# RWKV time mix: the low-rank inputs mixed by scaled factors, gates and decays between the wide projections

## The reference

```python
xx = _token_shift(h) - h
xr, xw, xk, xv, xa, xg = [h + xx * mu[i] for i in range(6)]
r, k, v = xr @ w_r, xk @ w_k, xv @ w_v                      # 1024 x 1024 each
w = -softplus(-(w0 + tanh(xw @ w1) @ w2)) - 0.5             # w1: 1024 x 64
a = sigmoid(a0 + (xa @ a1) @ a2)                            # a1: 1024 x 64
g = sigmoid(xg @ g1) @ g2                                   # g1: 1024 x 160
kk = heads(k * k_k); kk = kk / max(norm(kk), 1e-12)
k = k * (1 + (a - 1) * k_a)
decay = exp(-exp(w))
# scan over time with r, decay, k, v, -kk, kk * a; group norm over heads;
# plus sum(r * k * r_k) * v; times g; times w_o
```

## Time and profile before

| | |
|---|---|
| median of 3 runs | 1948.68 us (1945.17 to 1950.43) |
| the profiled execution's own time | 1943.3 us |
| its span in the trace | 1941.5 us |
| mean granted TensorE clock | 0.957 |
| RWKV part up to the head work | about 1462 to 1608 us of the span |

### The profile page before, as it was taken

How to read it: one execution, slowest core, us unless ns; L and a number is a source line. 1 busy time by engine, 2 the same in 40 slices (tenths; PEclk the granted TensorE clock), 3 DMA queues, 4 the chain that set the end, 5 groups by cost and what they waited for, 6 DMA issues and landing times.

```text
span 1941.5 us, 29831 instructions
## 1 busy us (share of the span) xinstructions
PE 1770.4 (91%) x12438; PEld 1271.5 (65%) x12438; DVE 917.8 (47%) x1344; ACT 672.9 (35%) x950; POOL 499.5 (26%) x362
## 2 busy tenths in 40 slices
PE   5989999999769999999999589889997979969998
PEld 2889997795534444444444366668885749958887
DVE  4286623677712112121222665464456775765553
ACT  3454347442301112111111344444334443334342
POOL 1268887100133445454453100000000001400000
PEclk9999999999879999999999788889998989999999
DMA  8545551166599998979888532155444500023442
GB/s 357 183 151 181 195 178 63 66 239 255 237 426 423 419 381 326 393 297 421 354 333 350 205 110 107 55 200 189 180 181 144 194 22 25 4 87 147 180 178 102
DMA packets 64970, 414.41 MB, mean 213 GB/s; under 512 B 20612, under 2 KB 20628, under 8 KB 24528
## 3 DMA queue, kind: packets, MB, share of 16 engines
q0 software_dynamic: 37808, 218.05, 27.9%
q1 hardware_dynamic: 26624, 192.95, 26.6%
q10 hardware_dynamic: 416, 1.66, 0.2%
HBM read 550.99 MB, written 2.10 MB: 285 GB/s over the span
## 4 chain that ended last, share of the span: by engine, by line
PE 78%; DVE 9%; DMA 6%; ACT 3%; issue 3%; POOL 1%; DVEq 0%; POOLq 0%; ACTq 0%
PE ps L1063 12%; PE ps L804 10%; PE ps L805 10%; PE ps L806 10%; PE ps L1082 6%; PE ps L842 4%; PE ps L840 4%; PE ps L841 4%; PE ps L1096 3%; PE ps L858 2%; PE ps L1429 2%; PE ps L1049 1%; DMA ring<-in_moe_dn,arena 1%; DMA spare<-in_moe_gu,arena 1%; DMA arena<-in_moe_dn,arena 1%
## 5 line engine op out<-in xcount | busy, mean ns | idle before, releaser
L805 PE MATMUL ps<-ring_lo,arena_r 128*128 128x512 f32 x888 | 355.0, 400 | 0.0
L1063 PE MATMUL ps<-arena 128*32 128x512 f32 (+2 forms) x832 | 244.3, 601 | 6.9 <-DMA spare<-in_moe_gu,arena 4.2
L804 PE MATMUL ps<-arena_r 128*128 128x512 f32 x528 | 211.3, 400 | 9.7 <-DVE arena_r L2227 9.7
L842 PE MATMUL ps<-arena_r,ring_lo 128*128 128x256 f32 x768 | 217.5, 283 | 0.0
L806 PE MATMUL ps<-arena_r 128*128 128x512 f32 x528 | 207.4, 393 | 0.0
L1063 PE MATMUL ps<-ring,arena 128*32 128x512 f32 (+2 forms) x560 | 201.7, 601 | 3.0 <-DMA ring<-in_moe_gu,arena 1.0
L805 PEld LDWEIGHTS ps<-ring_lo,arena_r 128*128 128x128 f32 x888 | 171.0, 193 | 35.6
L2201 DVE TENSOR_TENSOR ring_lo<-ring,arena_r 128x2048 fp32r<-128x2048 f32 x66 | 150.7, 2291 | 77.5 <-ACT arena_r L1617 77.3
L1617 ACT ACTIVATE high<-ring 128x2048 fp32r<-128x2048 f32 x62 | 118.6, 1917 | 125.7 <-PE ps L840 64.8
L840 PE MATMUL ps<-arena_r,high 128*128 128x256 f32 x528 | 148.9, 282 | 3.0 <-DVE ring_lo L2201 1.3
L2573 DVE SCALAR_TENSOR_TENSOR arena<-ps,arena 128x256 f32<-128x256 f32 x38 | 18.4, 484 | 280.7 <-ACT arena L1741 280.7
(11 more groups left out here) (457 smaller groups left out, 3627.1 us busy)
## 6 DMA issues: line engine op xcount, KB each, us to landing
ring<-in_weights SPq DMA_DIRECT2D x183, 1024.0 KB, 4.8
arena<-in_ln POOLq DMA_DIRECT2D x2, 1024.0 KB, 7.4
arena<-in_lora POOLq DMA_DIRECT2D x1, 1152.0 KB, 5.4
arena<-in_x POOLq DMA_DIRECT2D x1, 1024.0 KB, 12.3
h_rows<-arena ACTq DMA_DIRECT2D x1, 1024.0 KB, 12.7
arena<-in_bands POOLq DMA_DIRECT2D x1, 1024.0 KB, 11.7
arena<-in_rw_kk_ka POOLq DMA_DIRECT2D x2, 512.0 KB, 7.4
arena<-in_rw_w0a POOLq DMA_DIRECT2D x1, 1024.0 KB, 4.8
```

The costliest lines, as they stand in the source:

```text
L804: head = pe.matmul(dst, hi, w, start=start, stop=False, skip_group_check=True)
L805: pe.matmul(dst, hi, rest, start=False, stop=False, skip_group_check=True)
L842: mm = pe.matmul(dst, rest, hi[:, k, :], start=False, stop=(k == count - 1))
L1063: mm = pe.matmul(pb("moe", mu("gu", i))[at, :], x_cols[:, k, at], gu_w[s % SETS][:, k * 512:(k + 1) * 512], start=(k == 0), stop=(k == KC ...
```

## The change

The low-rank inputs no longer use variants. Since (h + mu * xx) @ W = h @ W + xx @ (mu * W), TensorE multiplies `hT` with the first factors and adds `shifted` times factors scaled by mu. GpSimd scales the factors ahead, in four products into `mixed_wag` (buf 7) and `mixed_g2`. lw and la become one unit (lwa); the 32-wide part of lg is summed in four column groups and added up by a further product, lg 2. These sums stand ahead of the projections. w2 stands after rw_r's first unit pair, L and PC after rw_k's first, a2 after rw_k's second, rw_v is last, and g2 comes behind the transposes artT, bT and kT. Copies, sigmoids and exponentials on the scalar engine are queued in the new order. The variants of r, k and v stay; the second variant moves from buf 7 to buf 13. The row `k_a` is fetched when rw_r 0 is full, the row `r_k` when `rw_tilde` is 3; its product now takes the scaled r and scaled k.

The new list of units, and GpSimd's part:

```diff
+       ("lwa", 1), ("lg", 3), ("rw_r", 4), ("w2", 4), ("rw_k", 4), ("L", 4), ("PC", 1), ("a2", 4), ("rw_v", 4),
+       ("artT", 8), ("bT", 4), ("kT", 4), ("g2", 4), ("rk", 117),
...
+    pool.wait_ge(sem("lora_in"), 64)
+    pool.wait_ge(sem(f"w_used{slot('ffn0', 29)}"), (TILES["ffn0"] + 29) // SLOTS + 1)
+    for dst, src, m in ((mixed_wag[:, :, 0:64], lora1[:, :, 0:64], 1), (mixed_wag[:, :, 64:128], lora1[:, :, 64:128], 4),
+                        (mixed_wag[:, :, 128:256], lora1[:, :, 128:256], 5), (mixed_g2, lora1[:, :, 256:288], 5)):
+        pool.tensor_tensor(dst, src, spread(p2("mu", KC, m * KC), src.shape[2]),
+                           ALU.mult).then_inc(sem("mixed"), 1)
     full(pool, "r0T", 3)
     row(buf(3), a["rw_w0a0"]).then_inc(sem("w0a0_in"), 16)
-    full(pool, "lg", 1)
-    row(buf(6)[:, 0:D], a["rw_kk_ka"][:, D:2 * D]).then_inc(sem("ka_rk_in"), 16)
-    row(buf(7)[:, 0:D], a["rw_rk"]).then_inc(sem("ka_rk_in"), 16)
+    full(pool, "rw_r", 0)
+    row(buf(10)[:, 0:D], a["rw_kk_ka"][:, D:2 * D]).then_inc(sem("ka_in"), 16)
+    pool.wait_ge(sem("rw_tilde"), 3)
+    row(buf(13)[:, 0:D], a["rw_rk"]).then_inc(sem("rk_in"), 16)
```

TensorE (only the new and kept lines; the removed ones are printed with the kernel above):

```diff
+    lora_sums(("lwa", 0), lora1[:, :, 0:128], hT, False, turned_part)
+    lora_sums(("lg", 0), lora1[:, :, 128:256], hT, False, turned_part)
+    lora_sums(("lg", 1), lora1[:, :, 256:288], hT, False, turned_part)
+    pe.wait_ge(sem("mixed"), 4)
+    lora_sums(("lwa", 0), mixed_wag[:, :, 0:128], shifted, True, shifted_part)
+    lora_sums(("lg", 0), mixed_wag[:, :, 128:256], shifted, True, shifted_part)
+    lora_sums(("lg", 1), mixed_g2, shifted, True, shifted_part)
+    stream("rw_r", 0, 0)
+    was_read(pe, "lg", 1)
+    two_parts("lg", 2, pb("lg", 2)[0:32, 0:T], const("sum4", HEADS), stacked)
+    was_read(pe, "lwa", 0)
     for i in range(4):
         cols, t = slice(i // 2 * 512, i // 2 * 512 + 512), i % 2
         small_product("w2", i, pb("w2", i), [(lora_wa[0:64, tokens(t)], lora2[0:64, cols])])
+    stream("rw_r", 0, 1)
+    stream("rw_k", 1, 0)
     pe.wait_ge(sem("logw"), 1)
     for i in range(4):
         cols, t = slice(i // 2 * 512, i // 2 * 512 + 512), i % 2
+        two_parts("L", i, pb("L", i), const("cum"), logw[:, t, cols])
     claim(pe, "PC", 0)
     for p in range(8):
         for t in range(NT):
             mm = pe.matmul(pb("PC", 0)[:, p * 4 + 2 * t:p * 4 + 2 * t + 2], logw[:, t, p * P:(p + 1) * P],
                            const("ind", 2), start=True, stop=True)
     filled(mm, "PC", 0)
+    stream("rw_k", 1, 1)
+    for i in range(4):
+        cols, t = slice(i // 2 * 512, i // 2 * 512 + 512), i % 2
+        two_parts("a2", i, pb("a2", i), lora_wa[64:128, tokens(t)], lora2[64:128, cols])
+    for u in range(2):
+        stream("rw_v", 2, u)
     pe.wait_ge(sem("rw_tilde"), 2)
...
+    all_read(pe, "lg", 3)
+    for i in range(4):
+        cols, t = slice(i // 2 * 512, i // 2 * 512 + 512), i % 2
+        small_product("g2", i, pb("g2", i), [(lora_g[:, tokens(t)], g2a[:, cols]),
+                                             (lora_g2[:, tokens(t)], g2b[:, cols])])
```

The scalar engine, in the same way:

```diff
+    def out_rows(stage, dst, i):
+        full(act, stage, i)
+        step.read(fn(dst[:, i % 2, i // 2 * 512:(i // 2 + 1) * 512], pb(stage, i), ACT.Copy), stage, i)
+
+    warm(ACT.Tanh)
     round_variant(0)
+    full(act, "lwa", 0)
+    step(fn(lora_wa[0:64, :], pb("lwa", 0)[0:64, 0:T], ACT.Tanh))
+    step.read(fn(lora_wa[64:128, :], pb("lwa", 0)[64:128, 0:T], ACT.Copy), "lwa", 0)
+    round_variant(1)
+    full(act, "lg", 1)
+    step.read(fn(stacked, pb("lg", 1)[:, 0:T], ACT.Copy), "lg", 1)
+    round_ahead("rw_r", 0, 12)
     warm(ACT.Sigmoid)
     full(act, "lg", 0)
     step.read(fn(lora_g, pb("lg", 0)[:, 0:T], ACT.Sigmoid), "lg", 0)
+    for i in range(2):
+        out_rows("rw_r", r_tok, i)
+    full(act, "lg", 2)
+    step.read(fn(lora_g2, pb("lg", 2)[0:32, 0:T], ACT.Sigmoid), "lg", 2)
+    round_ahead("rw_r", 1, 12)
     all_read(act, "w2", 4)
+    step(fn(buf(0), buf(0), ACT.Sigmoid), "w_sigmoid")
+    for i in range(2, 4):
+        out_rows("rw_r", r_tok, i)
+    round_variant(2)
+    round_ahead("rw_r", 2, 12)
+    for i in range(2):
+        out_rows("rw_k", k_hat, i)
+    round_ahead("rw_r", 3, 12)
     warm(ACT.Exp)
     for i in range(4):
         cols, t = slice(i // 2 * 512, i // 2 * 512 + 512), i % 2
         full(act, "L", i)
         act.wait_ge(sem("l_before"), i + 1)
         step(fn(p_cum[:, t, cols], pb("L", i), ACT.Exp))
         step.read(fn(p_inv[:, t, cols], pb("L", i), ACT.Exp, scale=-1.0), "L", i)
+    step(fn(buf(7), buf(7), ACT.Exp), "p_before")
     full(act, "PC", 0)
     step.read(fn(sml("G", 32), pb("PC", 0)[:, 0:32], ACT.Exp), "PC", 0)
+    for i in range(2, 4):
+        out_rows("rw_k", k_hat, i)
+    round_ahead("rw_r", 4, 12)
+    root(32)
+    warm(ACT.Sigmoid)
+    all_read(act, "a2", 4)
+    step(fn(buf(12), buf(12), ACT.Sigmoid), "a_sigmoid")
+    act.wait_ge(sem("ka_used"), 1)
+    for i in range(4):
+        out_rows("rw_v", v_rw, i)
+    act.wait_ge(sem("kk_done"), 1)
```

The vector engine (`half_variant` is four operations of the kind of L2726, `add_rows` four additions of a row of w0 or a0):

```diff
+    shift(0)
+    shift(1)
+    half_variant(0, 0)
+    half_variant(0, 1)
+    rest_of_variant(0, 0)
+    rest_of_variant(0, 1)
+    half_variant(1, 0)
+    half_variant(1, 1)
+    for half in range(2):
+        rest_of_variant(1, half)
+    rest_ahead("rw_r", 0, 12)
+    full(dve, "lwa", 0)
+    full(dve, "lg", 0)
+    full(dve, "lg", 1)
+    dve.wait_ge(sem("w0a0_in"), 16)
+    add_rows("w2", logw, 0)
+    rest_ahead("rw_r", 1, 12)
     dve.wait_ge(sem("w_sigmoid"), 1)
+    step(ts(buf(0), buf(0), -EXP_M_HALF, None, M), "logw")
+    full(dve, "rw_r", 3)
+    half_variant(2, 0)
+    half_variant(2, 1)
+    for half in range(2):
+        rest_of_variant(2, half)
+    rest_ahead("rw_r", 2, 12)
+    rest_ahead("rw_r", 3, 12)
     for i in range(4):
         cols, t = slice(i // 2 * 512, i // 2 * 512 + 512), i % 2
         full(dve, "L", i)
         step(tt(a_til[:, t, cols], pb("L", i), logw[:, t, cols], S), "l_before")
+    dve.wait_ge(sem("kk_in"), 16)
+    all_read(dve, "rw_k", 4)
+    step(tt(kk, k_hat, rows(b15[:, 0:D], NT), M))
+    step(tt(buf(12), buf(13), buf(13), M))
+    step(dve.tensor_reduce(sml("sq", 32), heads(buf(12)), AX_X, A))
+    step(ts(sml("sq", 32), sml("sq", 32), 1e-24, None, ALU.max), "root_asked")
+    add_rows("a2", a_tok, D)
+    rest_ahead("rw_r", 4, 12)
+    inverse_root(32)
+    step(tt(heads(buf(13)), heads(buf(13)), spread(sml("rs", 32), HD), M))
+    all_read(dve, "rw_r", 4)
     all_read(dve, "L", 4)
     step(tt(buf(8), buf(8), buf(4), M), "rw_tilde")
     dve.wait_ge(sem("p_before"), 1)
+    step(stt(out=buf(7), in0=buf(13), scalar=-1.0, in1=buf(7), op0=M, op1=M), "rw_tilde")
+    tmp = tok(buf(4))
+    dve.wait_ge(sem("ka_in"), 16)
+    dve.wait_ge(sem("a_sigmoid"), 1)
+    step(stt(out=tmp, in0=a_tok, scalar=-1.0, in1=rows(buf(10)[:, 0:D], NT), op0=A, op1=M), "ka_used")
+    step(stt(out=buf(9), in0=buf(4), scalar=1.0, in1=buf(9), op0=A, op1=M), "kk_done")
+    step(tt(buf(3), buf(13), buf(12), M))
     step(tt(buf(3), buf(3), buf(5), M), "rw_tilde")
     step(tt(buf(9), buf(9), buf(5), M), "rw_tilde")
+    rw_mask = const("rw", 2 * CH)
+    all_read(dve, "rw_v", 4)
+    dve.wait_ge(sem("rk_in"), 16)
+    step(tt(rkk, r_til, k_hat, M))
+    step(tt(rkk, rkk, rows(buf(13)[:, 0:D], NT), M))
```

More of the change, by code:

```diff
@@ L1347, in _, with stream @@
             turn_tile("r0T", 1)
[L1348 to L1351, removed]
+            def stream(stage, n, u):
+                product_tok(stage, (variant_hi[n % 2], variant_lo[n % 2]), 2 * u, 2 * u,
+                            ready=lambda half: pe.wait_ge(sem("variant_lo"), 2 * n + half + 1))
@@ L1359, in _ @@
[L1359 to L1363, removed]
+            def two_parts(stage, unit, dst, lhs, rhs):
+                if not late:
+                    small_product(stage, unit, dst, [(lhs, rhs)])
+                    return
+                claim(pe, stage, unit)
+                half = rhs.shape[1] // 2
+                carry(pe.matmul(dst[:, 0:half], lhs, rhs[:, 0:half], start=True, stop=True))
+                filled(pe.matmul(dst[:, half:], lhs, rhs[:, half:], start=True, stop=True), stage, unit)
@@ new lines, in lora_sums @@
+            def lora_sums(unit, w, moving, last, ready):
+                if not last:
+                    claim(pe, *unit)
+                m = w.shape[2]
+                for k in range(KC):
+                    ready(k)
+                    g = slice(32 * (k % 4), 32 * (k % 4) + 32) if m == 32 else slice(0, P)
+                    open_, close = (3, 4) if m == 32 else (0, KC - 1)
+                    mm = pe.matmul(pb(*unit)[g, 0:T], w[:, k, :], moving[:, k, :], start=not last and k <= open_,
+                                   stop=last and k >= close, skip_group_check=True)
+                    if k == 0:
+                        carry(mm)
+                if last:
+                    filled(mm, *unit)
@@ L2720, in _ @@
-            shift(0)
```

(34 more changed lines are left out.)

86 lines of the change are left out of this document (19 added, 67 removed).

## The result

The changed kernel takes 1958.41 us (median of 11 runs, 1952.67 to 1965.01); the kernel before took 1948.04 us beside it (11 runs, 1945.14 to 1959.23). The ratio is 1.0054, with a 95% interval from 1.0035 to 1.0073: 10.4 us slower, where +4.4 us was forecast. It is inside the stated range of 1945 to 1962 us, but just above the forecast's own bounds (1948 to 1958 us, +9.5 us at most), and it is the "slower" case (chance 0.31), not "no change" (0.56).

What follows compares the result with a forecast made beforehand. The part was taken as bound by TensorE first, then by a chain of elementwise work. The steps moved the vector engine's first masked product from 1609.06 to 1613.4 us, +4.4 us, giving 1953.1 us; range 1945 to 1962 us.

Steps and rivals of the forecast that it cites:

- own bounds: Forecast's range from favourable and unfavourable clock and row-landing assumptions: 1948 to 1958 us, about -1 to +9.5 us.
- "slower" case: Whole kernel: slower by more than can be told from no change (0.3%, 5.8 us); chance 0.31.
- no change: Whole kernel: difference too small to tell, forecast with a clock fall (0.34) or without (0.22); chance together 0.56.
- Step 1: Low-rank sums ahead of rw_r: 16.5 against 14.6 us, filling a 7.65 us wait; rw_r starts at 1488.6 us.
- Step 2: Inside w2: TensorE waits 3 us for lg 0's bank, its sigmoid queued behind tile 4's rounding; w2 ends at 1506.9 us.
- Step 3: L and PC between projections: PC waits 1 us, then 4.6 us at half clock; rw_k's second unit ends at 1551.2 us.
- Step 4: Inside a2: TensorE stands 12.8 us for the scalar engine's queued copy of rw_k 2; a2 ends at 1569.3 us.
- Step 5: Vector engine's chain from rw_k's copy, with 2.8 us waiting for r_k's row, ends at 1613.4 us, +4.4 us.
- Hidden terms: Shifts, half variants, four POOL products (about 5 us) and an extra dummy table load beside the sums: no added time.
- Slower by r_k's row: Before the masked products: late landing of r_k's row decides from 6.6 us on, 10.4 us giving +9.6; slower chance 0.31.
- Faster through an absent queue: At a2: without the scalar engine's queue TensorE alone sets the end, -20 us, 1928 us; faster chance 0.13.
- no fall after PC: Behind the PC block: clock stays up, everything after 2.1 us earlier, total +2.3 us, 1951 us; chance 0.22.

Runs made afterwards that it cites:

- e2: Changed kernel with the gate's sigmoids queued ahead of the rounding of tiles 3 and 4, the rw_r copies behind; ratio to the kernel before 0.9998.
- e9: Changed kernel with r_k's row fetched into the place of k_k's row as soon as that has been used; ratio to the kernel before 1.0026.
- e11: Changed kernel with only the PC block and its read on the scalar engine moved behind rw_v; ratio to the kernel before 1.0011.
- e1: Changed kernel with the copies of rw_k 2 and 3 queued between the roundings of tiles 9 and 10, ahead of the exponentials; ratio to before 0.9986.
- e5: Changed kernel with the edits of e1 and e2, plus L subtractions and exponentials queued ahead of tiles 9 and 10; ratio to before 0.9946.
- e3: Changed kernel with 25 added, overwritten matmuls keeping TensorE busy during a2's wait, scalar queue unchanged; ratio to the kernel before 1.0006.
- e6: e5 with the PC block moved behind rw_v; 1925.87 us, ratio to the kernel before 0.9901.
- e8: Kernel before with only the new low-rank sums ahead of rw_r and sigmoids queued early, other work behind the projections; ratio to before 0.9951.

## Why the prediction was right in its mechanism and short in its size

**Step 1, right.** The sums filled the wait. rw_r started at 1486.76 us where 1487.8 was forecast: the clock rose at 1472 us (0.95 in that slice), not 1474.5.

**Step 2, the term that failed.** The wait was right, 2.72 us for 3. I took its clock as unchanged and named a fall only as a bound. It fell, through w2 and 5.3 us into rw_r's second unit: 2.6 us more in w2 (5.31 us for six matmuls against 2.73) and twelve wide matmuls at 0.427 instead of 0.235 us, 2.3. Even with the earlier start, rw_k's first unit ended at 1532.8 us, 4.1 late. I had argued from 3.45 us of idle that left the clock at full; here 2.7 us did not. e2 confirms the price, 7.7 us for a wait of 2.72 us at the first L product; e9, with the same wait, paid 1.3 us less.

**Step 3, right and slightly dear.** The clock fell after PC (in e11, without the block there, it did not), for about 3.4 us where I took 4.6. rw_k ended 2.9 us late instead of 4.1.

**Step 4, right in place and length, its clock too small.** 12.46 us of standing for 12.8 forecast, by the queue that I wrote down (e1 and e5 take it apart); rw_k was copied at 1567.5 us, 3.1 late. Then a2 took 5.49 us, not 4.4, and rw_v's first half 8.5, not 5.7: the clock came back 11 us after the work. rw_v's first half ended 6.5 us late, and the vector engine's wait for tile 11 grew with it, to 5.17 us. e3 shows that the clock behind this wait is 4.9 us of the ruler, of which the forecast had only the part in a2 (4.4 us, partly slow).

**Step 5, right.** The eight operations took what was forecast, k was scaled 6.4 us late. r_k's row landed in 3.78 us rather than 5.2 and was waited for 1.87 us, not 2.8; the end came out 5.3 us late, at 1617.9 for 1612.6. That is the whole error: +9.7 where +4.4 was forecast. It is made up of 2.9 us from steps 1 to 3 (step 2's clock, less what steps 1 and 3 had too dear), 3.8 us of step 4's clock, and 1.1 us that the row gave back; 0.3 us are not told apart.

**Hidden terms, right.** The four POOL products ran at 1450 us (5.55 us), the shifts and variants were done before their use, and no second table load cost more than its 1.28 us plus dummy. The Trainium skill ("ScalarE: Activation LUTs", What ACT_TABLE_LOAD costs) has about 2.7 us; this trace agrees with the earlier trace rows instead: each load is 1.28 us with the next activation 0.01 to 0.02 us behind it, and the row was the better guide.

**The rivals.** Slower by r_k's row: the side was right, the mechanism wrong, since e9 finds about 1 us there. Faster through an absent queue: the queue was there, but what it would be worth without it was well put. I gave -20 us against before for TensorE alone, and e6, which takes the queue apart, is 17.1 us on the ruler and 18 us timed. That most of the 12.8 us must go before the change gains anything holds: e1 takes 8.3 us of 12.46 and ends level with before. The price that I gave, no fall after PC for 2.1 us, is near the 1.2 us that the slow matmuls cost there; e11's 7.8 us are mostly the block itself.

What went wrong is thus the weighing: step 2's clock loss stood only in the bounds, and a2's was counted in part. With step 2's 4.9 us in the sum it gives +9.3 us, which is slower. That this is so near the measured +9.7 is luck in part, since the rest of step 4's clock, missing as well, was offset by the terms that were too dear.

## What to carry to other kernels

Price a stall of TensorE with the slow matmuls behind it, not by its own length: here 2.72 us of standing cost 6.5 to 7.7 us, and 12.46 us cost 4.9 us more than themselves. Give that price a range: the same wait did not cost the same in every execution. When work is moved between projections, write down for each accumulation bank who frees it and what is queued ahead of that reader on its engine, and after curing one wait look for the next bank in the same queue (e1's 4.20 us). Put short reads that release a bank ahead of long work that nobody waits for; that alone turned a change of +0.54% into -0.43%, and with two further moves into -1%.

## What the runs showed of the hardware that I had not expected

The granted clock did not follow the work closely, and not in the same way in every execution. It stayed at 1.2 GHz through 5.31 us of w2 and 5.49 us of a2, both busy without a gap, and came back 5.2 and 5.5 us after the wide products had begun behind them; in e9, where the instructions up to there are the same, it came back 2.4 us after they had begun, in both places. It fell at the end of 2.72 us of standing in front of w2, and of 2.86 us in front of e8's head products, but held through 3.45 us of standing in the kernel before. It fell behind PC's 3.77 us of 2-column products in the changed kernel, though TensorE had stood only 0.41 us, and held behind the same block in e6.

Both slow blocks have operands of 64 rows, but that does not explain it. In the kernel before, 32 matmuls of the same shape run at full clock:

```profile
1564.35:1578.20 13.85, 13.85 (x32) 4.83 (x32) 11.87 (x12) 5.61 (x5) 0.63 (x2) 1.00 0.25 76
```

In e3, products of 128 rows and 256 columns in place of the standing kept the clock at full, and the same 64-row matmuls behind them ran at full too. What decides at which moment the clock falls and comes back was not tried by itself and stays open.
